# Differential attention on a Trainium2 core: one pass over the keys with kept exponentials, instead of two

## The reference

```python
def diff_block(qp, q):
    s = jnp.einsum('bqhmd,bkhmd->bhmqk', q.astype(f32), kd) * SCALE
    bias = table[t5_bucket(kpos[None, :] - qp[:, None])]
    s = s + jnp.transpose(bias, (2, 0, 1))[None, :, None]
    mask = (kpos[None, :] // CHUNK) <= (qp[:, None] // CHUNK)
    s = jnp.where(mask, s, NEG_INF)
    p = jax.nn.softmax(s, axis=-1)
    a = p[:, :, 0] - lam * p[:, :, 1]
    return jnp.einsum('bhqk,bkhe->bqhe', a, vd)
```

## Time and profile before

| | us |
|---|---|
| median of three executions | 2807.61 |
| profiled execution, span | 2803.1 |
| projection stage | 0 to about 1425 |
| prompt's attention, pass B of the first to the last head | 1425 to 2396 |
| merge | 2396 to 2803 |

### The profile page before, as it was taken

How to read it: one execution, slowest core, us unless ns; L and a number is a source line. 1 busy time by engine, 2 the same in 40 slices (tenths; PEclk the granted TensorE clock), 3 DMA queues, 4 the chain that set the end, 5 groups by cost and what they waited for, 6 DMA issues and landing times.

```text
span 2803.1 us, 37797 instructions
## 1 busy us (share of the span) xinstructions
PE 2697.1 (96%) x15257; PEld 2162.7 (77%) x15257; DVE 1184.0 (42%) x1847; ACT 1083.4 (39%) x2182; POOL 255.9 (9%) x270
## 2 busy tenths in 40 slices
PE   5999999999999999999989999999999999999998
PEld 4788888889999999999865665566566556888897
DVE  3421224315443332443333464365355446655554
ACT  3123331112122222100356676676666667422221
POOL 0100001131000000112230000000000003100000
PEclk9999999999999999999989999999999999999999
DMA  3453334448776766766651405053250503544442
GB/s 105 130 155 107 105 106 139 140 141 220 216 204 188 204 168 169 206 192 162 168 130 28 100 23 123 5 121 70 58 118 5 123 16 115 163 136 136 135 125 94
DMA packets 405774, 353.71 MB, mean 126 GB/s; under 512 B 45440, under 2 KB 368968, under 8 KB 399416
## 3 DMA queue, kind: packets, MB, share of 16 engines
q1 hardware_dynamic: 396464, 332.66, 44.1%
q0 software_dynamic: 9136, 18.63, 2.0%
HBM read 250.23 MB, written 100.71 MB: 125 GB/s over the span
## 4 chain that ended last, share of the span: by engine, by line
PE 86%; ACT 4%; DVE 3%; DMA 2%; issue 2%; POOL 1%; SPq 1%; DVEq 0%; ACTq 0%; POOLq 0%
PE p_acc L834 13%; PE p_acc L836 13%; PE p_acc L835 13%; PE a_sa L1887 5%; PE a_sa L1890 5%; PE a_sb L1907 4%; PE a_op L1936 4%; PE a_sb L1916 4%; PE a_op L1933 3%; PE p_turn L865 2%; PE e_U L1390 2%; PE e_U L1391 2%; PE e_U L1392 2%; ACT a_sa L1762 2%; ACT a_e L1791 2%
## 5 line engine op out<-in xcount | busy, mean ns | idle before, releaser
L834 PE MATMUL p_acc<-p_h_hi,p_w_hi 128*128 128x384 f32 (+1 forms) x1960 | 717.2, 366 | 9.8 <-DVE p_h_lo L652 5.8
L836 PE MATMUL p_acc<-p_h_hi,p_w_lo 128*128 128x384 f32 (+1 forms) x1960 | 702.0, 358 | 0.0
L835 PE MATMUL p_acc<-p_h_lo,p_w_hi 128*128 128x384 f32 (+1 forms) x1960 | 701.4, 358 | 0.0
L1813 DVE TENSOR_REDUCE a_nmax<-a_sa 128x1 f32<-128x1024 f32 (+7 forms) x384 | 349.4, 913 | 481.9 <-PE a_sa L1890 481.6
L1791 ACT ACTIVATE a_e<-a_sb 128x512 f32<-128x512 f32 (+3 forms) x640 | 317.9, 532 | 245.4 <-PE a_sb L1916 240.5
L834 PEld LDWEIGHTS p_acc<-p_h_hi,p_w_hi 128*128 128x128 f32 x1960 | 369.4, 188 | 45.2 <-issue 10.2
L836 PEld LDWEIGHTS p_acc<-p_h_hi,p_w_lo 128*128 128x128 f32 x1960 | 369.0, 188 | 31.5
L835 PEld LDWEIGHTS p_acc<-p_h_lo,p_w_hi 128*128 128x128 f32 x1960 | 369.8, 189 | 29.5
L1762 ACT ACTIVATE a_sa<-a_sa,a_nmax 128x1024 f32<-128x1024 f32 (+7 forms) x384 | 323.7, 843 | 73.3 <-DVE a_nmax L1813 71.9
L1887 PE MATMUL a_sa<-a_k,a_q 128*128 128x512 f32 (+4 forms) x640 | 261.6, 409 | 39.8 <-ACT a_sa L1762 33.3
L1907 PE MATMUL a_sb<-a_q,a_k 128*128 128x512 f32 (+2 forms) x640 | 272.5, 426 | 5.7 <-ACT a_e L1791 4.5
(11 more groups left out here) (217 smaller groups left out, 3490.4 us busy)
## 6 DMA issues: line engine op xcount, KB each, us to landing
p_raw<-in_w_in SPq DMA_DIRECT2D x98, 512.0 KB, 5.3
s_k_raw<-in_cache_fox_k SPq DMA_DIRECT2D x32, 512.0 KB, 6.9
s_v_raw<-in_cache_fox_v SPq DMA_DIRECT2D x32, 512.0 KB, 6.4
s_k_raw<-in_cache_diff_k SPq DMA_DIRECT2D x32, 512.0 KB, 7.1
s_v_raw<-in_cache_diff_v SPq DMA_DIRECT2D x32, 512.0 KB, 6.6
a_q<-scratch_q_hi SPq DMA_DIRECT2D x32, 512.0 KB, 13.8
a_k<-scratch_k_hi SPq DMA_DIRECT2D x32, 512.0 KB, 12.5
e_pair<-scratch_gT SPq DMA_DIRECT2D x80, 192.0 KB, 2.7
```

The lines of the kernel that those rows point to most:

```text
L834: nc.tensor.matmul(acc[a % 2][:, 0:n], hi, h_hi[p][:, k, at:at + n], start=(k == 0), stop=False)
L835: nc.tensor.matmul(acc[a % 2][:, 0:n], hi, h_lo[p][:, k, at:at + n], start=False, stop=False)
L836: last = nc.tensor.matmul(acc[a % 2][:, 0:n], lo, h_hi[p][:, k, at:at + n], start=False, stop=(k == DK - 1))
L1813: nc.vector.tensor_reduce(nmax[:, b % 2, c, col:col + 1], scores_of(ev[1]), axes, ALU.max, negate=True).then_inc(a_maxed, 1)
```

## The change

- Differential heads have no pass B any more. Pass A's exponentials go to SBUF: map 0 into `w`, a ring of 7936 columns, map 1 into `e1`.
- When both maps of a query tile are done (D steps), VectorE works out per query and chunk the coefficients 1/sum and -lambda/sum, corrected for the chunk's own maximum. GpSimd multiplies `w` by the first in place, VectorE adds `e1` times the second. The weights are thus combined with queries on the partitions.
- They are then turned, 128x128 at a time (`turn`), for half blocks of 256 queries and key units of 256 keys, into pass B's PSUM banks. ScalarE copies them to `wT`, and TensorE multiplies with the values in two matmuls of 256 columns. There are 36 such units per differential head.
- Forgetting heads keep both passes. Their products are now issued three units at a time, for two before.
- The planner paces by estimated microseconds instead of units (`F_LEAD`, `D_LEAD`, `BEHIND`, `SHARE`), and holds pass A of a tile back while its place in `w` isn't turned yet.
- Differential heads load five map parts per map instead of six (`k2` is shared by both maps) and the band in one layout. The loads are issued at other points of the list.
- The merge's early steps move: squares, means and y steps stand three or four slots later. SP and GpSimd wait for pass B of the forgetting heads (`pair_done`) before the merge's first loads and memsets.

```diff
-        slots[23] += [("SQ", 0, 0)]
-        slots[24] += [("SQ", 0, 1)]
-        slots[25] += [("MN", 0, 0)]
-        slots[26] += [("MN", 0, 1)]
+        slots[26] += [("SQ", 0, 0)]
+        slots[27] += [("SQ", 0, 1)]
+        slots[29] += [("MN", 0, 0)]
+        slots[30] += [("MN", 0, 1)]
         for j in range(8):
-            slots[27 + j] += y_step(0, j)
-        slots[29] += [("MN", 0, 2)]
-        slots[30] += [("MN", 0, 3)]
+            slots[31 + j] += y_step(0, j)
+        slots[33] += [("MN", 0, 2)]
+        slots[34] += [("MN", 0, 3)]
...
+                att["pair_done"](sp)
                 sp.dma_start(gcol, d["subln_g"].rearrange("a p -> p a")).then_inc(const_in, 16)
-                att["pair_done"](sp)
...
             if ev_[0] == "I":
+                link["attention"]["pair_done"](pool)
                 nc.gpsimd.memset(eps, EPS).then_inc(const_set, 1)
...
+    W_COLS = 7936
+    HALVES = SEQ // HALF_Q
...
-        maps.append([[s.sb(f"{n}_1{m}", [P, SEQ], F32R) for m in range(MAPS)] for n in ("q1", "k1", "q2", "k2")])
-        q1, k1, q2, k2 = ([maps[f][n] for f in range(2)] for n in range(4))
-        e = s.sb("e", [P, E_SLOTS, MAPS, QUERIES])
-        w = s.sb("w", [P, W_SLOTS, QUERIES])
+        dq1, dk1 = ([s.sb(f"{n}_1{m}", [P, SEQ], F32R) for m in range(MAPS)] for n in ("q1", "k1"))
+        dk2 = s.sb("k2_1", [P, SEQ], F32R)
+        w = s.sb("w", [P, W_COLS])
+        e1 = s.sb("e1", [P, 2, SEQ])
+        v.append(s.sb("v1", [P, PROMPT_TILES, P]))
         o = s.sb("o", [P, 2, QUERIES])
-        v.append(s.sb("v1", [P, PROMPT_TILES, P]))
-        band = s.sb("band", [P, 2, 3, BAND], BF16)
+        wT = s.sb("wT", [P, T_SLOTS, 2 * HALF_Q])
+        band = s.sb("band", [P, 3, BAND], BF16)
+        e_b = s.sb("e_b", [P, 3, MAPS, QUERIES])
...
+    A_UNITS, B_UNITS = [], []
+    for pair in range(PAIR_N):
+        for Q in range(BLOCKS):
+            for t in range(4):
+                for m in range(MAPS):
+                    A_UNITS += [("f", pair * BLOCKS + Q, m, t, c) for c in range(1 + Q // 2)]
+        for i in range(PROMPT_TILES):
             for m in range(MAPS):
-                for c in range(1 + Q // 2):
-                    A_UNITS.append((b, m, t, c))
-        B_UNITS += [(b, kt) for kt in range(4 * Q + 4)]
...
+        for Q in range(BLOCKS):
+            B_UNITS += [("f", pair * BLOCKS + Q, kt) for kt in range(4 * Q + 4)]
+        for h in range(HALVES):
+            B_UNITS += [("d", pair * HALVES + h, j) for j in range(h + 1)]
...
-    LEAD = 9
-    STEP = 300
-    a_work = list(itertools.accumulate([0] + [a_width(unit) + STEP for unit in A_UNITS]))
-    RATE = 1.04 * a_work[NA] / NU
-    FINISH = ["X", 0, 1, 2, None, None, 3, 4]
+        return 16 * (3 if f % 2 else 2) * (f // 2 + 1)
+
+    F_LEAD, D_LEAD = 16.0, 9.0
+    BEHIND, SHARE = 6.0, 1.4
+    a_us = [2 * a_width(a) / 2250 + 0.25 for a in range(NA)]
+    b_us = []
+    for kind, n, k in B_UNITS:
+        if kind == "f":
+            b_us.append((QUERIES - max(0, k - 4 * (n % BLOCKS)) * P) * 8 / 2250)
+        else:
+            b_us.append(1.28 if k < n % HALVES else 0.9)
+    a_work = list(itertools.accumulate([0] + a_us))
+    b_time = list(itertools.accumulate([0] + b_us))
+    RATE = 1.04 * a_work[NA] / b_time[NB]
+    FINISH = [0, 1, 2, None, None, 3, 4]
...
+            unit = A_UNITS[a]
+            if unit[0] == "f":
+                return [("F", unit[1], n) for n in FINISH]
+            y = unit[1]
+            return [("D", unit[:2], k) for k in range(0 if two_d(y) else 2, 5)]
...
+                if unit[0] == "d" and unit[2] == 0 and w_after[unit[1], unit[3]] > turned:
+                    return
+                if done == a_first[unit[:2]]:
+                    if unit[0] == "f":
+                        flush([unit[1] - 2, ("d", unit[1] // BLOCKS * PROMPT_TILES - 1)])
+                    else:
+                        flush([("d", unit[1] - 2)])
...
+        for n, unit in enumerate(B_UNITS):
+            kind, g, k = unit
+            if n == b_first[unit[:2]]:
+                for _ in pass_a(a_end[kind, g] + 1):
+                    stages(1)
+                for _ in pass_a(NA):
+                    stages(1)
+                    if now > ended.get((kind, g), 0.0) + BEHIND:
+                        break
+                flush([g] if kind == "f" else [("d", 2 * g), ("d", 2 * g + 1)])
+            if kind == "f" and g % BLOCKS == 1 and k == 0 and g > BLOCKS:
+                out.append(("L", 2 * (g // BLOCKS) + 1))
+            if kind == "d" and g % HALVES == 0 and g // HALVES + 1 < PAIR_N:
+                out.append(("L", 2 * (g // HALVES) + 2))
+            out += [("B", unit), ("E", unit)]
+            if kind == "d" and n == b_last[unit[:2]]:
+                turned = g
+            now += b_us[n]
+            share = pass_a(min(target(n), next(a for a in range(done, NA + 1) if a == NA or a_work[a] > a_work[done] + SHARE * b_us[n])))
+            if not finish and not scored:
                 next(share, None)
             stages(1)
-            if u >= 2 and is_diff(B_UNITS[u - 2][0]):
-                multiply(u - 2)
-            elif u >= 3 and u % 2:
-                multiply(u - 3)
-                multiply(u - 2)
+            if kind == "d" or pending and pending[0][0] == "d" or len(pending) > 3:
+                while len(pending) > 1:
+                    multiply()
+            pending.append(unit)
             for _ in share:
                 stages(1)
-            if b // BLOCKS == FT - 1:
-                out += [("MERGE", ev) for ev in link["merge"]["early"].get(u - b_first[NB - BLOCKS], [])]
-        out.append(("W", NU - 1))
-        multiply(NU - 2)
-        multiply(NU - 1)
+            if len(finish) > 10:
+                stages(1)
+            if n >= NB - ND:
+                out += [("MERGE", ev) for ev in link["merge"]["early"].get(n - (NB - ND), [])]
+        while pending:
+            multiply()
+        early = link["merge"]["early"]
+        out += [("MERGE", ev) for n in sorted(early) if n >= ND for ev in early[n]]
...
+    def weights_of(a):
+
+
+        _, y, m, c = A_UNITS[a]
+        at, width = c * CHUNK_KEYS, a_width(a)
+        dst = e1[:, y % 2, at:at + width] if m else w[:, w_off[y, c]:w_off[y, c] + width]
+        return dst if width <= 512 else dst.rearrange("p (b n) -> p b n", b=2)
...
+            elif ev[0] == "D" and ev[2] == 3:
+                y = ev[1][1]
+                pool.wait_ge(d_dve, dd_at[y, "coef"])
+                pool.wait_ge(a_summed, a_last["d", y] + 1)
+                for c in range(1 + two_d(y)):
+                    part, _ = w_chunk(y, c)
+                    nc.gpsimd.tensor_scalar(part, part, coef[:, y % 2, c, 0:1], None, ALU.mult).then_inc(w_scaled, 1)
...
+                if is_diff(a):
+                    _, y, m, c = A_UNITS[a]
+                    if m == 0:
+                        g = w_after[y, c]
+                        if g >= 0:
+                            act.wait_ge(w_turned, d_at[g, g % HALVES] + 1)
+                        if y >= 4 and c == 0:
+                            act.wait_ge(d_dve, dd_at[y - 4, "coef"])
+                    elif (m, c) == (1, 0) and y >= 2:
+                        act.wait_ge(w_made, w_at[y - 2, int(two_d(y - 2))])
+                    nc.scalar.activation(weights_of(a), scores_of(a), ACT.Exp, bias=dmax[:, y % 4, c, m:m + 1],
...
+            elif ev[0] == "E":
+                unit = ev[1]
+                n = d_at[unit[1:]]
+                act.wait_ge(w_turned, n + 1)
+                if n >= T_SLOTS:
+                    act.wait_ge(d_mult, n - T_SLOTS + 1)
+                if unit[2] < unit[1] % HALVES:
+                    nc.scalar.copy(wT[:, n % T_SLOTS, :], sb_[n % 2][:]).then_inc(wT_made, 1)
+                else:
+                    nc.scalar.copy(wT[:, n % T_SLOTS, 0:HALF_Q], sb_[n % 2][:, 0:HALF_Q])
+                    nc.scalar.copy(wT[:, n % T_SLOTS, HALF_Q + P:], sb_[n % 2][:, HALF_Q + P:]).then_inc(wT_made, 1)
...
+            elif ev[0] == "D":
+                y, step = ev[1][1], ev[2]
+                r, z = y % 4, y % 2
+                if step == 0:
+                    dve.wait_ge(a_maxed, a_last["d", y] + 1)
+                    nc.vector.tensor_tensor(dm[:, z, :], dmax[:, r, 0, :], dmax[:, r, 1, :], ALU.min).then_inc(d_dve, 1)
+                    dve.wait_ge(d_dve, dd_at[y, "min"])
+                    nc.vector.tensor_tensor(dgap[:, z, 0, :], dm[:, z, :], dmax[:, r, 0, :], ALU.subtract)
+                    nc.vector.tensor_tensor(dgap[:, z, 1, :], dm[:, z, :], dmax[:, r, 1, :], ALU.subtract).then_inc(d_dve, 1)
+                elif step == 1:
+                    dve.wait_ge(d_act, d_act_at[y])
+                    dve.wait_ge(a_summed, a_last["d", y] + 1)
+                    nc.vector.tensor_tensor(dls[:, z], dgap[:, z], dsum[:, r], ALU.mult).then_inc(d_dve, 1)
+                    dve.wait_ge(d_dve, dd_at[y, "scale"])
```

(58 more changed lines are left out.)

521 lines of the change are left out of this document (299 added, 222 removed).

## The result

The changed kernel takes 3096.3 us (3093.2 to 3098.3 in four runs), the kernel before 2807.5 (2803.7 to 2809.3) beside it: ratio 1.103, interval 1.1015 to 1.1046. Forecast were 2767 us, with a range of 2712 to 2814: the prediction was wrong, in sign as well as in size. The profiled execution has a span of 3096.2 us.

The account below looks back on a forecast made before the run. TensorE was taken to set the pace. Span 2803.1 - 155.4 (pass B scores) + 72.4 (turns) + 33 (hand-offs) + 9 (merge) = 2762 us; with 4.5 us from span to median, 2767 us, range 2712 to 2814.

Parts of the forecast that it names:

- Pass A of the differential heads writes SBUF instead of PSUM: nothing.: Differential heads' pass A: writing its exponentials to SBUF instead of PSUM was to cost nothing.
- I cost them at nothing: Map and band loads on SP's queue: issued some 70 us ahead of first use, so no cost.
- one landing of 13.8 us per pair: Loads: about what they would cost per pair without the cover of being issued early.
- 98 us: Differential stretch: 98 us after the change for 112 before, with VectorE at 91%.
- the term: Hand-offs between engines in the four differential stretches: +33 us in sum, ends 0 and +81.
- Forgetting stretches held at 130: Forgetting heads' stretches: held constant at 130 to 131 us, 128 to 134 expected.
- rival 3: GpSimd's scale of the weights is slow, decisive from 1.7 ns a column: +96 us, 2863 us, chance 0.10.
- The collision: Second chunk's GpSimd scale against the first chunk's VectorE combination: 1.05 us each, 8.4 us per pair.
- the exclusion for a whole instruction: VectorE with two SBUF inputs and GpSimd reading SBUF exclude each other; a scale could wait up to 1.3 us.
- rival 4: TensorE's clock falls to 1.2 GHz in differential stretches: +62 us in each of four, about 3015 us, chance 0.02.
- the merge's steps: Merge's first y steps at the end: some 9 of 16 us stand bare, +9 us, ends 4 and 14.
- rivals 1 and 2: Differential stretches: 1, TensorE keeps the pace, 2734 us, chance 0.17; 2, hand-offs hurt more, 2806 us, chance 0.13.

Follow-up runs that it names:

- e15: As e11, but the second product of a differential head's pass A over the map's own 64 rows again: 2912.1 us, ratio 1.0375.
- e11: As e10, with the merge's first steps four slots earlier: 2811.9 us, ratio 1.0022.
- e7: As e3, with the second product of a differential head's pass A over all 128 rows: 2932.3 us, ratio 1.0433.
- e3: Changed kernel with the scale on ScalarE instead of GpSimd and loads issued one part per pass B unit: 3034.4 us, ratio 1.0794.
- e6: Kernel before, with the second product of a differential head's pass A over 64 rows instead of 66: 2909.5 us, ratio 1.0356.
- e2: Changed kernel with the next pair's loads issued one part per pass B unit instead of all at once: 3050.9 us, ratio 1.0862.
- e10: As e7, with the work reordered (empty steps before the combination, pass A ahead of products), other planner numbers and two list thresholds changed: 2817.5 us, ratio 1.0043.
- e13: As e11, with a longer lead for forgetting heads' pass A, other planner numbers, empty steps' places and products kept back also changed: 2802.3 us, ratio 0.998.
- e8: As e7, with the planner's BEHIND (work between a block's pass A and its first pass B unit) 2.0 instead of 6.0: 2923.4 us, ratio 1.0416.
- e1: Changed kernel with the scale of map 0's weights on ScalarE instead of GpSimd: 3084.2 us, ratio 1.098.

## Why the prediction was wrong, point by point

- **"Pass A of the differential heads writes SBUF instead of PSUM: nothing."** This is the step that failed, and the largest single edit's worth. It looked at where the exponentials go and not at the operands of its matmuls, which the diff changed from 66 rows to 64. It cost 100 us (e15 against e11) or 102 (e7 against e3), and the same edit costs the kernel before 100 (e6: 2909.5 against 2809.8 beside it). The trace of before has no product over 64 rows at all; a part whose operand shapes change has to be bounded like a new operation.
- **The loads, "I cost them at nothing".** I had counted when the loads must land, not what is queued behind them on SP. The stores were; 45 us (e2). The kernel before loads in the same burst, but behind the store of the last forgetting block and not ahead of it. The other end I gave, one landing of 13.8 us per pair, is near the 16.8 of the wait in size only: it was a landing that TensorE would wait for, not a store.
- **"98 us" a differential stretch, for the hand-offs.** Here the mechanism, queues that wait for one another, was right and the size was off. VectorE's busy time came out near what was worked out, but the planner's order keeps scale, combination, maxima and exponentials in one file, so that the queues lose 115 us (e10 against e7, forgetting stretches included) where the term held 33 for all of it. In the best order the stretch is 97 us, by the windows of e13 (differential, forgetting):

```profile
1814.00:1911.00 97.00, 85.57 (x474) 67.65 (x470) 58.53 (x117) 65.85 (x141) 2.05 (x4) 0.95 0.37 88
1911.00:2056.00 145.00, 136.27 (x619) 76.97 (x617) 68.37 (x126) 96.50 (x213) 6.14 (x12) 0.94 0.23 53
```

  That this meets my 98 is luck: VectorE is busy 60% of it and not 91, since part of the work that I had put there now stands in the forgetting stretch.

- **Forgetting stretches held at 130.** They rose to 146 in the changed kernel, with hardly more of pass A in them (VectorE busy 54 us), and to 145 in e13, where VectorE has 126 operations and is busy 68 us, for 78 and 52 before. A pair takes 242 us in e13 against 243 before (112 and 131) and 228 in the forecast: what the differential stretch gives, the forgetting one takes back. At its head three pass A units stand with little between them. Further on pass B waits for the rows of constants to land. The chain in e13:

```profile
1914.70 0.50 PE a_sa L2122
1915.20 0.24 PE a_sa L2128
1915.44 0.24 PE a_sa L2122
1915.68 0.25 PE a_sa L2128
1915.96 1.24 DVE a_nmax L2007
1917.24 0.99 issue
1918.47 0.50 PE a_sa L2122
...
1950.33 9.31 DMA a_q<-a_c_lo
```

  And the clock behind that wait, by windows:

```profile
1940.00:1960.00 20.00, 17.61 (x84) 9.72 (x85) 9.60 (x17) 13.38 (x30) 2.05 (x4) 0.98 0.91 193
1960.00:1980.00 20.00, 20.00 (x58) 11.83 (x58) 6.19 (x6) 9.42 (x17) 0.00 (x0) 0.59 0.39 93
```

  A unit at the head takes 3.8 us with 1.2 of TensorE in it, at a clock of 1.00. Of the 9.31 us of landing TensorE stands idle for only 2.4, but then it is busy for 20 us at 0.59; by my estimate (0.41 x 20) that is 8 us. Bursts and clock are both candidates for the last 35 us to my forecast. e8, which shortened the bursts in e7's order, gained 9 us, and no run took either away in e13's order, so it stays open.
- **GpSimd's scale (rival 3).** Its condition came true (2.8 ns a column, above 1.7), its price of 96 us didn't: on ScalarE the scale gave back 12 to 16 us, left out 64. VectorE waited 98.8 us for it in all, eight times what e1 gained: where the queues are in a bad order, another wait takes the place of the one removed, and ScalarE takes 45 us for the 1024-column forms of the same work. The collision that I had priced at 1.05 us a time is there, but smaller: a combination of 1024 columns takes 1579 ns in the mean in the changed kernel and 1307 in e3, where GpSimd has no scales. The longest scale takes 2.85 us for a mean of 2.84, so none was held up by a combination. And one combination (1713.44, 2.06 us) starts and ends within two scales on end (1710.49 to 1716.15), so the exclusion for a whole instruction that the prediction quotes isn't borne out there, as far as the spans of GpSimd are exact.
- **The clock (rival 4).** It fell to 0.83 in the differential stretches, 0.94 over the run. In the rows shown it falls behind gaps in TensorE's work (10 us at 1620 above; 2.4 us of waiting just before 1960 in e13), and e10, e11 and e13, with as many turns, have 0.97 to 0.98 over the run, 0.95 in the stretch shown above. The rule of the Trainium skill on turns (TensorE: Matmul & The Clock Gate, "Part 4: PE-mode transpose") isn't needed for any of these rows; in e13 the 20 us from 1840, amid the turns, stand at 1.00. But no run took the turns away. That rival 4's 3015 us come nearest to the 3096 measured says nothing for it: rows, loads and order gave back 235 us without touching the turns.
- **Right:** a turn takes 0.11 us (four in 0.44 in e7's chain, 0.133 assumed); the product's price is unchanged, 0.86 us for the four passes of a unit; the merge's steps stood bare for about 6 us in the changed kernel, from the last product's end at 2679.3 to the unbroken row of merge matmuls at 2685.2 (9 forecast).

```profile
1957.35 0.44 PE a_sb L2167 x4
...
1957.89 0.86 PE a_op L2194 x4
```

- **The range** held the forecast and rivals 1 and 2, each taken alone; rival 3 (2863) lay outside it. Three misses of 45 to 115 us fell on the same side, and two of them were terms set to nothing, with no end in the range.
